# Attention units' second copies on ScalarE, the head norm by quarters, the compressed mask folded, X by four transfers, and warm-up products on 64x64 quarters

## What is computed

```python
mix = token_mixing(x, w_in[l], ...)              # conv branch, differential attention, three-way sparse attention
x = layer_norm(ALPHA * x + mix, ln1_g[l], ln1_b[l])
ffn = conv_ffn(x, ffn_w_up[l], ...)
x = layer_norm(ALPHA * x + ffn, ln2_g[l], ln2_b[l])
```

```python
p_cmp = jax.nn.softmax(jnp.where(cvalid, sc, NEG), axis=-1) * cvalid
o_cmp = jnp.einsum('bghsn,bngd->bsghd', p_cmp.astype(vc_c.dtype), vc_c)
```

## Time and profile before

| | |
|---|---|
| Median of 3 runs | 3649.57 us (3646.88 to 3649.74) |
| The profiled execution's own time | 3648.67 us |
| Its span, first to last instruction | 3646.7 us |
| Mean granted PE clock | 0.991 |
| PE busy | 3539.7 us, 97% |
| DVE, ACT, POOL busy | 1744.6, 1353.4, 1270.6 us |
| The largest group, L2829 on POOL (remainders of chunks) | 504 times 2458 ns |
| L474, L475, L476 on PE, the split products | some 390 to 400 ns each, started some 0.23 us apart |
| The chain that ended last | issue 44%, PE 36%, POOL 17% |

### The profile page before, as it was taken

One profiled execution on the slowest core, in us unless ns is written; L12 is line 12 of the kernel. 1 busy time (PEld: TensorE's weight loads), 2 busy tenths in 40 slices (PEclk: granted clock), 3 DMA queues, 4 the chain that ended last, 5 costly groups with the idle time before them and its releaser, 6 DMA issues.

```text
span 3646.7 us, 52307 instructions
## 1 busy us (share of the span) xinstructions
PE 3539.7 (97%) x19658; PEld 2749.3 (75%) x19658; DVE 1744.6 (48%) x2651; ACT 1353.4 (37%) x2300; POOL 1270.6 (35%) x602
## 2 busy tenths in 40 slices
PE   8999999999999999999999999999999998999998
PEld 7877687888788767788877677788854597767886
DVE  2656657443345664754335642604147665435042
ACT  3234523332323453333325544423225143444232
POOL 4422243444443223444443143344300012424442
PEclk9999999999999999999999999999999999999999
DMA  3421122222223111222222222222222301212222
GB/s 138 126 75 48 52 81 87 98 98 104 90 100 117 51 53 67 84 92 97 99 98 96 101 98 70 86 94 98 104 98 71 92 4 42 93 64 93 98 98 81
DMA packets 101269, 313.21 MB, mean 86 GB/s; under 512 B 26592, under 2 KB 26720, under 8 KB 100192
## 3 DMA queue, kind: packets, MB, share of 16 engines
q1 hardware_dynamic: 81792, 298.90, 23.6%
q10 hardware_dynamic: 19296, 11.76, 1.3%
HBM read 302.23 MB, written 5.24 MB: 84 GB/s over the span
## 4 chain that ended last, share of the span: by engine, by line
issue 44%; PE 36%; POOL 17%; DVE 1%; ACT 1%; DMA 1%; POOLq 0%; DVEq 0%; SPq 0%; ACTq 0%
POOL ring_r L2829 17%; PE ps L474 9%; PE ps L475 9%; PE ps L476 9%; PE ps L1157 2%; PE ps L1081 1%; PE ps L836 1%; PE ps L1010 1%; PE ps L1036 1%; DMA ring<-in_weights 0%; PE ps L1194 0%; PE ps L1183 0%; PE ps L1111 0%; PE ps L1266 0%; POOLq L2828 0%
## 5 line engine op out<-in xcount | busy, mean ns | idle before, releaser
L2829 POOL TENSOR_TENSOR ring_r<-ring,rounded_r 128x1024 fp32r<-128x1024 f32 x504 | 1237.2, 2458 | 1967.2 <-ACT rounded_r L1338 1966.8
L474 PE MATMUL ps<-source_hi,rounded_r 128*128 128x512 f32 x2560 | 1024.1, 400 | 41.6 <-issue 11.8
L1338 ACT ACTIVATE rounded_r<-ring 128x1024 fp32r<-128x1024 f32 x504 | 533.1, 1058 | 1303.5 <-PE ps L476 1180.6
L475 PE MATMUL ps<-source_hi,ring_r 128*128 128x512 f32 x2560 | 1001.6, 391 | 0.0
L474 PEld LDWEIGHTS ps<-source_hi,rounded_r 128*128 128x128 f32 x2560 | 483.8, 189 | 170.6 <-issue 30.8
L476 PE MATMUL ps<-X_lo,rounded_r 128*128 128x512 f32 x1536 | 602.3, 392 | 0.0
L475 PEld LDWEIGHTS ps<-source_hi,ring_r 128*128 128x128 f32 x2560 | 484.1, 189 | 96.3 <-issue 2.4
L476 PEld LDWEIGHTS ps<-X_lo,rounded_r 128*128 128x128 f32 x1536 | 290.2, 189 | 62.4
L476 PE MATMUL ps<-N_lo,rounded_r 128*128 128x512 f32 x768 | 299.2, 390 | 0.0
L2368 DVE SCALAR_TENSOR_TENSOR T<-ps,PAR,T 128x511 f32<-128x511 f32 (+1 forms) x176 | 131.5, 749 | 227.3 <-ACT T L1570 211.0
L474 PE MATMUL ps<-H_hi,rounded_r 128*128 128x512 f32 x512 | 199.2, 389 | 0.0
(11 more groups left out here) (489 smaller groups left out, 5275.0 us busy)
## 6 DMA issues: line engine op xcount, KB each, us to landing
ring<-in_weights SPq DMA_DIRECT2D x560, 512.0 KB, 3.2
X<-in_x SPq DMA_DIRECT2D x2, 1024.0 KB, 7.1
PAIR<-Z ACTq DMA_DIRECT2D x32, 64.0 KB
out_x<-X SPq DMA_DIRECT2D x4, 512.0 KB, 2.6
SWAP<-Z ACTq DMA_DIRECT2D x4, 256.0 KB, 6.0
MEM<-in_mem ACTq DMA_DIRECT2D x1, 1024.0 KB, 4.7
mem_keys<-Z ACTq DMA_DIRECT2D x1, 1024.0 KB, 3.9
diag_in<-Y ACTq DMA_DIRECT2D x8, 128.0 KB, 2.2
```

The lines of the kernel that those rows point to most:

```text
L474: mm(o, lh, rh, start=start, stop=False)
L475: mm(o, ll, rh, start=False, stop=False)
L1338: av(RH[:, j, :], ring[:, j, :], ACT.Copy).then_inc(w_hi, 1)
L2829: nc.gpsimd.tensor_tensor(RL[:, j, :], ring[:, j, :], RH[:, j, :].bitcast(F32), ALU.subtract).then_inc(w_lo, 1)
```

## The change

- A diff unit's second head is copied by ACT too, right behind the first; DVE copies only the odd heads of sparse units. `copy_at` says which copy of which engine holds a head, `copy_before` which copy a bank must wait for; the semaphores' values follow.
- ACT squares YB tile by tile in units 8 to 11, DVE sums each tile behind units 9 to 12, and multiplies YB tile by tile behind units 18 to 21. The root stays in unit 16, the reciprocal behind unit 17.
- The four products of CS with `cvalid` are left out. Instead the factor of a row is multiplied by the mask of block 0: where block 0 is valid, masked blocks have exp(NEG) = 0 already.
- X comes by four transfers of two tiles instead of two of four, and ACT waits for each.
- DVE first clears RS; in layer 0 PE waits for this, runs four 128x512 products of RS with itself into bank 7, which nobody reads, and takes the first quad with one lane instead of two.
- Ahead of the RWKV units the two full-array products give way to 24 products of 64 columns and 16 of 128, each on one of the four 64x64 quarters, in banks 6 and 7, which nobody reads.

```diff
+def copy_at(l, u, i):
+
+    if UNITS[u][0] == "diff":
+return "act", l * 2 * NU + 2 * u + i + 1
+    if i % 2 == 0:
+return "act", l * 2 * NU + 2 * u + i // 2 + 1
+    return "dve", l * 2 * (NU - U_SEL) + 2 * (u - U_SEL) + i // 2 + 1
+
+
+def copy_before(l, u, i):
+
+    if i >= 2:
+return copy_at(l, u, i - 2)
+    if u > 0:
+return copy_at(l, u - 1, HEADS_OF[u - 1] - 2 + i)
+    return copy_at(l - 1, NU - 1, 2 + i) if l > 0 else None
...
-x_in = [sem(f"x_in{h}") for h in range(2)]
+x_in = [sem(f"x_in{h}") for h in range(4)]
+zeros = sem("zeros")
...
     for j in range(RING):
         sp.dma_start(ring[:, j, :], a["weights"][j]).then_inc(landed[j], 16)
         if j < 2:
-            half = slice(j * KT // 2, (j + 1) * KT // 2)
-            sp.dma_start(X[:, half, :], a["x"][:, half, :]).then_inc(x_in[j], 16)
+            for h in (2 * j, 2 * j + 1):
+                two = slice(2 * h, 2 * h + 2)
+                sp.dma_start(X[:, two, :], a["x"][:, two, :]).then_inc(x_in[h], 16)
...
+    def copied(at):
+
+        pe.wait_ge(at_pta if at[0] == "act" else at_ptd, at[1])
...
-        elif copies_before(l, u, i) > 0:
-            pe.wait_ge(at_ptd if i % 2 else at_pta, copies_before(l, u, i))
+        elif copy_before(l, u, i) is not None:
+            copied(copy_before(l, u, i))
...
-                pe.wait_ge(at_ptd if i % 2 else at_pta, copies_before(l, u, i) + 1)
+                copied(copy_at(l, u, i))
...
-            pe.wait_ge(at_pta, copies_before(l, u, 2) + 1)
-            pe.wait_ge(at_ptd, copies_before(l, u, 3) + 1)
+            copied(copy_at(l, u, 2))
+            copied(copy_at(l, u, 3))
...
-        first_quad(W0, 0, XH, XL, x_ready, l * 16, 2, (zc, l * C_Z), 2 if l == 0 else RING - 1)
+        if l == 0:
+            pe.wait_ge(zeros, 1)
+            for _ in range(4):
+                mm(ps[:, 7, :], RS[:, 0:P], RS[:], start=True, stop=True)
+        first_quad(W0, 0, XH, XL, x_ready, l * 16, 2, (zc, l * C_Z), 1 if l == 0 else RING - 1)
...
-            pe.wait_ge(at_pta, copies_before(l, u, 0))
-            pe.wait_ge(at_ptd, copies_before(l, u, 1))
+            for i in range(2):
+                copied(copy_before(l, u, i))
...
-            pe.wait_ge(yb_step, l * 4 + 4)
+            pe.wait_ge(yb_step, l * 7 + 7)
...
     decay_grams(0)
-    warm(7, 2, CST2)
+
+    def warm_quarters(n, cols):
+
+        for _ in range(n):
+            for bank, cross in ((6, 0), (7, HD)):
+                for r in (0, HD):
+                    c = r ^ cross
+                    mm(ps[c:c + HD, bank, 0:cols], CST2[r:r + HD, 0:HD], CST2[r:r + HD, 0:cols], start=True, stop=True)
+
+    warm_quarters(6, HD)
+    warm_quarters(4, P)
     blocks_below(0)
     key_grams(0)
     inverse(0)
...
     for j in range(RING - 1):
         round_chunk(0, j)
         if j < 2:
-            act.wait_ge(x_in[j], 16)
             for n in range(j * KT // 2, (j + 1) * KT // 2):
+                if n % 2 == 0:
+                    act.wait_ge(x_in[n // 2], 16)
                 av(XH[:, n, :], X[:, n, :], ACT.Copy).then_inc(src_hi, 1)
...
             turned(u, 0)
+            if not nsa:
+                turned(u, 1)
             if more:
                 exps(u + 1, 2)
             if nsa:
@@ -1515,14 +1552,16 @@
...
-            if u == U_SEL + 3:
-                act.wait_ge(at_out, l * NU + U_SEL)
-                av(SCR[:, 0:4, :], YB.rearrange("p t h d -> p t (h d)"), ACT.Square).then_inc(yb_step, 1)
+            if U_SEL <= u < U_SEL + ST:
+                t = u - U_SEL
+                if t == 0:
+                    act.wait_ge(at_out, l * NU + U_SEL)
+                av(SCR[:, t, :], YB[:, t].rearrange("p h d -> p (h d)"), ACT.Square).then_inc(yb_step, 1)
...
             if u == U_SEL + 8:
-                act.wait_ge(yb_step, l * 4 + 2)
+                act.wait_ge(yb_step, l * 7 + 5)
                 av(MS[:, 1, :], MS[:, 0, :], ACT.Sqrt, bias=cst("eps"), scale=1.0 / P).then_inc(yb_step, 1)
...
+    v.memset(RS[:], 0.0).then_inc(zeros, 1)
     for n in range(KT):
         dve.wait_ge(src_hi, n + 1)
         remainder(XL[:, n, :], X[:, n, :], XHF[:, n, :], x_ready, 2)
...
             v.tensor_reduce(CM[:, 1, :], csf, AXX, ALU.add)
             dve.drain()
-            for qi in range(ST):
-                tt(CS[:, qi], CS[:, qi], cv[:, qi].unsqueeze(1).to_broadcast([P, NH, NCMP]), ALU.mult)
             v.reciprocal(CM[:, 2, :], CM[:, 1, :])
             dve.drain()
             dve.wait_ge(gsig, l + 1)
             c2, c3 = [CM[:, i, :].rearrange("p (t h) -> p t h", t=ST) for i in (2, 3)]
             tt(c3, c2, GSIG[:, :, 0, :], ALU.mult)
+            dve.drain()
+            tt(c3, c3, cv[:, :, 0:1].to_broadcast([P, ST, NH]), ALU.mult)
             dve.drain()
             tt(csf, csf, CM[:, 3, :].unsqueeze(2).to_broadcast([P, ST * NH, NCMP]), ALU.mult).then_inc(cs_step, 1)
...
@@ -2304,27 +2344,32 @@
                 factors(l, u + 1, 0)
             if U_CS <= u < U_SEL:
                 compressed_output(u - U_CS)
-            turned(l, u, 1)
             if UNITS[u][0] != "diff":
+                turned(l, u, 1)
                 turned(l, u, 3)
             if u + 1 < NU:
                 factors(l, u + 1, 1)
             outputs(l, u)
             if u + 2 < NU:
                 maxima(l, u + 2)
-            if u == U_SEL + 4:
-                dve.wait_ge(yb_step, l * 4 + 1)
-                v.tensor_reduce(MS[:, 0, :], SCR[:, 0:4, :].rearrange("p t (h d) -> p (t h) d", h=DH), AXX, ALU.add).then_inc(yb_step, 1)
+            if U_SEL < u <= U_SEL + ST:
+                t = u - U_SEL - 1
+                dve.wait_ge(yb_step, l * 7 + t + 1)
+                ins = v.tensor_reduce(MS[:, 0, t * DH:t * DH + DH], SCR[:, t, :].rearrange("p (h d) -> p h d", h=DH), AXX, ALU.add)
+                if t == ST - 1:
+                    ins.then_inc(yb_step, 1)
             if U_SEL + 5 <= u < U_SEL + 9:
                 c = u - (U_SEL + 5)
                 dve.wait_ge(y_hi, l * Y_N + c + 1)
                 remainder(YLs[c], Y[:, c, :], YH[c].bitcast(F32), y_lo)
             if u == U_SEL + 9:
-                dve.wait_ge(yb_step, l * 4 + 3)
+                dve.wait_ge(yb_step, l * 7 + 6)
                 v.reciprocal(MS[:, 1, :], MS[:, 1, :])
-                dve.drain()
-                ybf = YB.rearrange("p t h d -> p (t h) d")
-                tt(ybf, ybf, MS[:, 1, :].unsqueeze(2).to_broadcast([P, ST * DH, P]), ALU.mult).then_inc(yb_step, 1)
+            if U_SEL + 9 < u <= U_SEL + 9 + ST:
+                t = u - U_SEL - 10
+                ins = tt(YB[:, t], YB[:, t], MS[:, 1, t * DH:t * DH + DH].unsqueeze(2).to_broadcast([P, DH, P]), ALU.mult)
+                if t == ST - 1:
+                    ins.then_inc(yb_step, 1)
         for c in range(4):
             dve.wait_ge(y_hi, l * Y_N + 4 + c + 1)
             remainder(YLs[8 + c], YC[:, c, :], YH[8 + c].bitcast(F32), y_lo)
```

More of the change, by code:

```diff
@@ L163 @@
 NHEADS = HEADS_BEFORE[NU]
+U_SEL = DH // 2 * ST
+U_CS = U_SEL - ST
 def half_done(l, u, i):
     return 2 * (l * NU + u) + (i if UNITS[u][0] == "diff" else i // 2) + 1
-def copies_before(l, u, i):
-    return (l * NHEADS + HEADS_BEFORE[u] + i) // 2
+def copy_at(l, u, i):
[10 more added lines that the diff above has]
+    return copy_at(l - 1, NU - 1, 2 + i) if l > 0 else None
 def readers_before(l, u):
     return l * NU + (max(u - 1, 0) if UNITS[u][0] == "diff" else u)
-U_SEL = DH // 2 * ST
-U_CS = U_SEL - ST
 NGATE = 3 * KT
```

## The result

The changed kernel takes 3623.52 us (median of 4 runs, 3622.28 to 3627.78), the kernel before in the same comparison 3649.65 (3646.88 to 3651.64): ratio 0.993, 95% interval 0.9918 to 0.9942, so 26.1 us faster. The profiled execution is a run of 3622.86 with a span of 3621.0.

A forecast was written before the change was run, and what follows sets the result against it. PE, busy 97%, bounds the kernel; its idle and low-clock time can be won. Gains of 14.5 and 7.4 less 1.2 and 0.5 make 20.2 us, so 3648.7 becomes 3628.5, median 3629; 8 in 10: 3622 to 3638, own range 3624 to 3634.

The forecast's parts named there:

- Copies and mask, 14.5 + 0: Unit 2, both layers: ACT's copies remove waits and slow stretches, 14.5 us gained; the folded mask, off PE's path, counts 0.
- The 0.3 per layer for scores(5): Attention after unit 2: scores(5) may wait 0.3 us for exps(4), taken off the gain once per layer.
- Norm by quarters, 7.4: Attention head norm: 5.6 us of waits and slow clock removed, 1.9 added; net 3.7 per layer, 7.4 in all.
- the 1.9 per layer for eight pieces: Head norm on DVE: eight 0.69 us pieces, each ahead of a copy, cost 1.9 us per layer, ends 0.5 and 4.0.
- Rival 1: Head norm: every piece delays a copy PE needs, 4 to 5.6 us per layer come back, time 3636; chance 0.17.
- the slow stretch of 1.7: Behind the last transpose wait, 411.1 to 414.6: the half-speed clock goes, 1.7 us gained per layer.
- The start, -1.2: Layer 0's first quad: one lane instead of two loses 1.2 us, ends 1.9 gained and 3.0 lost.
- the end of the last X_lo: Kernel start: DVE's last X_lo ends at 16.3 to 19.1, so the first quad ends at 33.4 to 36.2.
- rival 2: Start and RWKV warm-up: X_lo slips ahead of POOL, quad ends at 33.4, four quarters overlap; 3 us better, 3626; chance 0.14.
- RWKV warm-up, -0.5: Ahead of the RWKV units: quarter products take 1.6 to 3.2 us for 1.7; 0 to 1.5 lost, 0.5 taken.
- The bank rule: RWKV warm-up: row quarters sharing a bank take turns, 6.0 us for 1.7, 4.3 lost, time 3633; chance 0.04.
- rival 4: RWKV units: without full-array products the clock falls; decides from some 40 us, all 140 cost 70, to 3700; chance 0.03.

The follow-up runs named there:

- experiment 3: Changed kernel with the head norm in whole passes over 2048 columns again, as before the change; 3630.68 us.
- Experiment 12: Changed kernel with all X ahead of the second weight chunk, two unread start products, Y's fourth remainder six units later; median 3621.32 us, ratio to before 0.9922.
- 2: Changed kernel with the four products of CS with the mask back in place of the one small product; 3629.71 us.
- number 6: Changed kernel without any unread product ahead of the RWKV units; 3623.35 us.
- 7: Changed kernel with the 40 RWKV warm-up products all on the two diagonal quarters; products 3.18 us, grams to blocks below 4.17, whole time not given.
- 10: Changed kernel with the earlier two full-array products ahead of the RWKV units; grams to blocks below 2.94 us, whole time not given.
- number 11: Changed kernel with two unread 128x512 products after each of four groups of compressed scores, both layers; 3632.53 us.

## Why the prediction was right, and where it wasn't

Faster came, and 3623.5 lies in the range of 3622 to 3638, near its low end; the forecast's own range, 3624 to 3634, it missed by half a microsecond. That is 26.1 us against the 20.2 of the sum. Term by term, each measured on one or a few traces:

- **Copies and mask, 14.5 + 0: measured 17.1** (25.1 less 8.0). The mechanism was right to the row: both waits of 4.7 gone, the clock at 1.00 behind unit 2. Three things were off. The 0.3 per layer for scores(5) didn't come. The slow stretches behind the waits were priced by their busy part, 5.5 and 6.2 us, while the record of the clock has 6.8 each. And the waits of 0.8 and 1.4 of unit 1's scores on ACT, in the trace of before but not priced, are missing after; since they come and go, they are no part of the change. Without them, and without the 1.45 in experiment 3, what is left for copies and mask is 16.3. The mask was rightly called a cover, but a cover that isn't used costs 0; this one costs 1.4 alone, and without the copies' move it is worth 2.7 of a 4.7 us wait.
- **Norm by quarters, 7.4: measured 8.0.** The removed side is the 8.0, or 6.6, of experiment 3. The added side failed as a step: that one 0.69 us remainder at 398.27 made a wait of 0.51 took the operation nearest ahead of the copy for its cause. Experiment 12 moved it and the wait stayed. With it fell the ground of the 1.9 per layer for eight pieces; what is seen besides that wait is 0.4 in layer 0 and 0.7 in layer 1. Rival 1, built on the same reading, fell too. That the sum came out close is partly luck: too much was taken off for the pieces, and the slow stretch of 1.7 was counted as certain in both layers, while experiment 3 had it in one.
- **The start, -1.2: measured +0.6 to +1.4.** The path was right: product 0 can't end before the last X_lo, and 24 steps stand behind it. Even the old end, 35.3, was right (35.2). What failed is the size of one term, the end of the last X_lo. It was put at 16.3 to 19.1, and a loss of 1.2 takes it from the later half; it came at 15.9 in the kernel after and at 15.1 to 17.4 in the eight traces with this start. So product 0 ended at 17.0 and the quad at 33.3 (32.5 to 34.8), where "near 36" was expected, and the long gap of PE, 2.25 us, stood ahead of the fifth step and not of the last. The upper end of the term, 3.0 lost, doesn't follow from its own numbers either: 36.2 and 1.7 are 2.6 above 35.3. The slow stretch for which up to 1.7 was allowed came in five of these eight traces (2, 3, 6, 7 and 10), not in the kernel after. Of rival 2 this half came true. The traces show what POOL's remainders do to X_lo: four took 3.82 us partly beside one, 5.61 beside two, and eight took 5.09 with hardly any. The Trainium skill's page GPSIMD Engine Reference (Specifications) says that the SBUF interface is shared with VectorE, with contention for VectorE instructions with two SBUF inputs; these rows agree.
- **RWKV warm-up, -0.5: measured +0.3.** The products' own time came out at the lower end, 1.70 us: four quarters ran at once. But the range for the loss began at 0, and 0.3 was gained, since the quarter products could begin beside the last grams; that step had no term.
- **The bank rule.** Taking turns would have made it 6.0 us. Different row quarters wrote different partitions of the same bank at the same time here, 80 records in 1.70 us, and 3.18 with two quarters. The Trainium skill's page TensorEngine Tiling (Array Packing), Gotcha 1, says that different row tiles cannot access the same PSUM bank simultaneously; for these products the runs don't bear it out.
- **The clock in the RWKV units** stayed at 1.00 throughout, and dropped for only 3.4 us behind a wait of 2.9 (number 6). That is far from rival 4's 40 us.
- The sum of the terms, 17.1 + 8.0 + 0.6 + 0.3 = 26.0, is close to the 26.1 of the medians. It is no proof of the single terms: 17.1 is what 8.0 leaves of 25.1, and each rests on traces that scatter by 1 to 2 us.

## What to carry to other kernels

An operation that stands just ahead of a late one isn't yet its cause: before pricing an added piece by such a row, follow the late operation's own inputs back, here to another engine's exps. Two edits that shorten the same wait are priced together and not by undoing one at a time; undone singly they showed 7.7 of 17.1 us. A slow stretch that follows a wait in one trace need not follow it in the next, so price it with a chance of its own. And that a DVE operation began just before POOL's instead of just behind it was worth more (1.9 us) than the work that was cut to get it there (1.1), so look at what a shorter chain meets next.

## What was not expected of the hardware

- Matmuls on all four 64x64 quarters ran together at 21 ns a record although they shared banks: 1.70 us for 80, against 3.18 on two quarters.
- PE ran at 1.2 GHz while it was busy throughout: 13.7 us in layer 0 of number 11, with eight unread full-array products among the 64-row ones with 31 columns, and 6.8 or 10.2 in the traces without them. A wait of 2.09 us was followed by a slow stretch in layer 0 of number 3, its twin of 2.08 in layer 1 was not, and neither was the one of 2.25 us ahead of the second half of X in the kernel after, while in five other traces with the same start the clock fell there.
- The same tensor_scalar on 128x256 took 0.35 us when it began before POOL's remainder and 1.58 to 2.35 when it began behind it. In all 28 such cases of the fourteen traces it ended 0.14 to 0.16 us behind the remainder, as if it had waited for it: what it costs is what is left of POOL's operation.
